# Eight unread matmuls after each post-norm sum, taken out of a one-core transformer kernel

## What is computed

```python
for l in range(DEPTH):    # DEPTH = 2
    h = h + 0.5 * rmsnorm(swiglu(rmsnorm(h, g_pre_ffn1[l]), w_ffn1_gu[l], w_ffn1_down[l]), g_post_ffn1[l])
    mix = token_mixer(rmsnorm(h, g_pre_mix[l]), ...)
    h = h + rmsnorm(mix, g_post_mix[l])
    h = h + 0.5 * rmsnorm(swiglu(rmsnorm(h, g_pre_ffn2[l]), w_ffn2_gu[l], w_ffn2_down[l]), g_post_ffn2[l])
```

## Time and profile before

| | us |
|---|---|
| median of three runs | 2387.8 |
| lowest, highest | 2387.32, 2390.79 |
| the profiled execution | 2391.2 |
| its span | 2389.7 |
| TensorE busy | 2335.6 (98%) |
| VectorE busy | 1629.8 (68%) |
| ScalarE busy | 1232.2 (52%) |
| mean granted clock of TensorE | 0.993 of full speed |
| HBM traffic | 159 GB/s over the span |

### The profile page before, as it was taken

How to read it: one execution, slowest core, us unless ns; L and a number is a source line. 1 busy time by engine, 2 the same in 40 slices (tenths; PEclk the granted TensorE clock), 3 DMA queues, 4 the chain that set the end, 5 groups by cost and what they waited for, 6 DMA issues and landing times.

```text
span 2389.7 us, 45375 instructions
## 1 busy us (share of the span) xinstructions
PE 2335.6 (98%) x18642; PEld 2283.4 (96%) x18642; DVE 1629.8 (68%) x2889; ACT 1232.2 (52%) x2050; POOL 61.8 (3%) x114
## 2 busy tenths in 40 slices
PE   8999999999999999999999999889999999989999
PEld 7999999999999999999999999889999999978999
DVE  6655987775486569788656875766765767574764
ACT  5444555554454445655445654555544645455542
POOL 2000200000000011000000000000000010000000
PEclk9999999999999999999999999899999999999999
DMA  7654634475556555447655655535755676533753
GB/s 200 186 177 127 169 98 124 131 194 177 169 159 177 177 148 131 106 142 189 186 188 160 185 187 155 141 89 142 201 187 171 181 200 191 158 93 89 203 187 132
DMA packets 583438, 382.77 MB, mean 160 GB/s; under 512 B 19977, under 2 KB 559091, under 8 KB 583232
## 3 DMA queue, kind: packets, MB, share of 16 engines
q1 hardware_dynamic: 580080, 376.78, 54.5%
q0 software_dynamic: 3152, 3.08, 0.5%
HBM read 378.67 MB, written 1.07 MB: 159 GB/s over the span
## 4 chain that ended last, share of the span: by engine, by line
PE 86%; DVE 8%; ACT 3%; issue 2%; DMA 1%; SPq 0%; DVEq 0%; ACTq 0%
PE bank L607 85%; DVE wlo L2040 1%; ACT whi L1347 1%; DVE ry L2059 1%; DVE ry L2057 1%; DVE a_qk L2602 0%; PE bank L938 0%; DVE ybuf L2090 0%; DVE smh L2476 0%; DMA wraw<-in_w_ffn_gu 0%; DVE hT L2094 0%; PE bank L706 0%; DMA wraw<-in_ffn_w_up 0%; DVE xlo L2073 0%; DVE ssum L2052 0%
## 5 line engine op out<-in xcount | busy, mean ns | idle before, releaser
L2040 DVE TENSOR_TENSOR wlo<-wraw,whi 128x1024 fp32r<-128x1024 f32 (+1 forms) x713 | 863.7, 1218 | 278.3 <-ACT whi L1347 274.3
L1347 ACT ACTIVATE whi<-wraw 128x1024 fp32r<-128x1024 f32 (+1 forms) x713 | 744.5, 1052 | 581.6 <-DMA wraw<-in_w_ffn_gu 168.5
L607 PE MATMUL bank<-xhi,whi 128*128 128x256 f32 (+2 forms) x3880 | 576.9, 288 | 7.3 <-ACT whi L1347 3.6
L607 PE MATMUL bank<-xhi,wlo 128*128 128x256 f32 (+2 forms) x3880 | 564.0, 285 | 6.1 <-DVE wlo L2040 6.1
L607 PE MATMUL bank<-xlo,whi 128*128 128x256 f32 (+2 forms) x3880 | 554.0, 284 | 0.0
L607 PEld LDWEIGHTS bank<-xhi,whi 128*128 128x128 f32 (+1 forms) x3880 | 511.1, 189 | 18.3 <-ACT xhi L1385 5.8
L607 PEld LDWEIGHTS bank<-xhi,wlo 128*128 128x128 f32 (+1 forms) x3880 | 509.6, 189 | 9.4 <-DVE wlo L2040 9.0
L607 PEld LDWEIGHTS bank<-xlo,whi 128*128 128x128 f32 (+1 forms) x3880 | 504.7, 188 | 0.2
L607 PE MATMUL bank<-act_hi,wlo 128*128 128x256 f32 (+1 forms) x1408 | 400.6, 284 | 0.0
L607 PE MATMUL bank<-act_lo,whi 128*128 128x256 f32 (+1 forms) x1408 | 400.5, 284 | 0.0
L607 PE MATMUL bank<-act_hi,whi 128*128 128x256 f32 (+1 forms) x1408 | 398.6, 283 | 0.0
(11 more groups left out here) (419 smaller groups left out, 1828.1 us busy)
## 6 DMA issues: line engine op xcount, KB each, us to landing
wraw<-in_w_ffn_gu SPq DMA_DIRECT2D x176, 512.0 KB, 3.9
wraw<-in_w_ffn_down SPq DMA_DIRECT2D x88, 512.0 KB, 3.2
wraw<-in_ffn_w_gate SPq DMA_DIRECT2D x88, 512.0 KB, 3.8
wraw<-in_ffn_w_up SPq DMA_DIRECT2D x88, 512.0 KB, 3.8
wraw<-in_ffn_w_down SPq DMA_DIRECT2D x88, 512.0 KB, 3.2
wraw<-in_w_in SPq DMA_DIRECT2D x80, 512.0 KB, 3.9
wraw<-in_a_w_in SPq DMA_DIRECT2D x26, 512.0 KB, 3.9
wraw<-in_w_out SPq DMA_DIRECT2D x16, 512.0 KB, 3.8
```

The source lines that it names most:

```text
L607: return E.matmul(out_, lhsT, rhs, start=first, stop=last, skip_group_check=True)
L1347: A.activation(flat(whi, u), flat(wraw, u), ACT.Copy).then_inc(S("hi"), 1)
L2040: V.tensor_tensor(flat(wlo, u), flat(wraw, u), flat(whi, u).bitcast(F32), ALU.subtract).then_inc(lo_ready[u % RING], 1)
```

## The change

The eight matmuls and the wait ahead of them are taken out of `stat`, with their constant. The sums themselves and all other instructions stay.

```diff
@@ -26,7 +26,6 @@
 RING = 7
 SLOT = 1024
 LEAD = 4
-AWAKE = 8
 HEAD = 4
 TAIL = 3
@@ -639,11 +638,6 @@
                 m = mm(bank[b][:, 0:n], C("mean1024"), sqb[:, 1, 0:n], False, True)
             m.then_inc(S("stat"), 1)
             c.norm += 1
-            if after is not None:
-
-                E.wait_ge(S("y"), KD * after + 2)
-                for _ in range(AWAKE):
-                    mm(bank[1][:, 0:n], C("mean1024"), C("ones")[:, 0:n], True, True)
 
         def head(slabs, x, fill, stat_at=None):
```

## The result

| | before | with the change |
|---|---|---|
| median, us | 2388.32 (4 runs, 2387.32 to 2390.79) | 2400.22 (4 runs, 2399.53 to 2402.09) |
| ratio, 95% interval | | 1.0044 [1.0033, 1.0056] |
| profiled execution, its span | 2391.2, 2389.7 | 2402.09, 2400.7 |
| mean granted clock | 0.993 | 0.986 |

The kernel is slower by 11.9 us (0.5%) in the medians and by 11.0 us in the span of the profiled execution. Forecast were 2399 us and +10.7. The change was run once more with the experiments, on another chip: 2402.08 against 2389.67 (21 runs), ratio 1.0050 [1.0038, 1.0063].

A forecast was written before the change was run, and what follows sets the result against it. TensorE was taken to bound the kernel, with 86% of the chain. Six low-clock stretches, 6 × 4.2 × 0.447 = 11.3, less 0.6, gave +10.7 us on the 2387.8 median: 2399 us, range 2394 to 2404.

The forecast's parts named there:

- The removed work is worth 0: At six post-norms, 48 unread matmuls, some 22.6 us of TensorE, lie hidden under the ScalarE and VectorE chain: 0 us.
- A fall at all six: At each of six post-norms, the new TensorE idle of 4.1 to 4.6 us drops the clock to 1.2 GHz.
- two waits that lost the clock: TensorE's waits for a_qm inside the mixers, 5.0 and 3.4 us, both followed by granted clock 0.5.
- 4.2 us of low work each: After each post-norm's idle, TensorE works 4.2 us at the low clock, the middle value taken.
- the long and the short kind: Low-clock stretches last about 6.8 or 3.4 us; expected work left after the idle: 5.0, or 3.4 or less.
- 0.447 a microsecond: Each microsecond of head work at the low clock loses 0.447 us, from eight matmuls taking 1.70 against 0.94 us.
- Heads are bound by TensorE, mixer heads give back 0.3: At low clock TensorE lags ScalarE's xhi supply, so heads lose time; two heads leading into mixers regain 0.3 us each.
- The clock didn't hold: Rival for the six post-norm idles: the clock stays at its upper level, price 0, 2388 us; chance 8%.
- The mixers absorbed next to nothing: Rival: two late heads leading into mixers cost nothing, so four post-norms pay 7.5 us, 2395.3 us; chance 12%.
- the third rival: Long low stretches at all post-norms, 5.0 to 6.8 us of low work: +12.8 to +17.6, 2400.6 to 2405.4 us; 15%.
- The signs: Expected in the profile after: long xhi waits, low clock reaching into the heads, wider matmul spacing, heads 1.5 to 2.5 us longer.

The follow-up runs named there:

- e5: Twelve unread matmuls instead of eight at each post-norm, against the kernel before the change; 2395.05 us, ratio 1.0027.
- e1: Four unread matmuls instead of eight at each post-norm, against the kernel before the change; 2390.78 us, ratio 1.0007.
- e8: Two unread matmuls instead of eight, waiting for ScalarE's Exp in mid-idle at each post-norm, against the kernel before the change; 2397.03 us, ratio 1.0036.
- e3: Eight unread matmuls kept behind the four FFNs, left out behind the two mixers, against the kernel before the change; 2391.91 us, ratio 1.0008.

## Why the prediction was right

- *The removed work is worth 0.* Right. All six heads start on the same wait for xhi, and the chain under it is as long as before. Its slack was larger than read, since the length of a merged row holds the last matmul's end (e5).
- *A fall at all six.* Right, in both profiles of the change. The reason behind it, that idles of 4.1 to 4.6 us lie between two waits that lost the clock, was good enough for this size. As a rule for shorter ones it fails: e1 with idles of 2.2 us or more and e8 with 1.1 and 1.75 us come out the other way round.
- *4.2 us of low work each*: the term that was undersized. It was 5.8, 4.7, 5.9, 5.8, 3.0 and 3.1 us, 4.75 in the mean. The choice between the long and the short kind in equal parts got four long ones to two. And the long ones lost less of themselves to the idle than said: the clock fell 2.3 to 3.1 us after the engine had stopped, not 2.5 at each, so they left 5.6 us of work in the mean instead of 5.0. In time: 12.7 instead of 11.3.
- *0.447 a microsecond.* Right. The heads are longer by 11.64 us, and 28.5 × 0.447 less 0.6 is 12.1. The factor of one half of the Trainium skill ("TensorE: Matmul & The Clock Gate", Terms), put on the same low work, would have given 13.7, further off.
- *Heads are bound by TensorE, mixer heads give back 0.3.* Right: 2.24 and 2.26 us of loss where the low work alone says 2.61.
- *Rivals.* The clock didn't hold. The mixers absorbed next to nothing: from the first mixer head's end to the next post-norm's head it took 222.28 us before (239.12 to 461.40) and 222.01 with the change (241.67 to 463.68), 0.3 us of a loss of 2.2; in the second mixer it was less than 0.1 us. Long stretches, said to be everywhere in the third rival, came at four of six.
- *What was luck.* The low work was sized too small by 1.4 us in sum, and the heads then lost 0.5 us less than it makes, and the rest of the kernel 0.6 less. So +10.7 stands closer to the +11.0 of the span than its terms do. The +12.4 of the second measurement, with more runs of the kernel before, is further off and still within the +9 to +13 that the forecast named.
- *The signs.* Six waits of about 4 us came with 24.6 us in sum (some 26 said), the mean clock at 0.986 (0.987 said), heads longer by 1.3 to 2.6 us (1.5 to 2.5 said), and 0.23 us between matmul starts with 272 columns (0.21 said).

## What to carry to other kernels

An engine that idles off the critical path can still cost, if its clock follows its work: before removing work that nobody reads, look at the granted clock behind waits of similar length in the same trace. Where TensorE bounds the stage after a dependency chain, a little filler under the chain pays. It needn't fill the wait: here four matmuls in the middle, 1.8 us from start to start, did as much as eight with 3.5 us; two were too few. And once such a price is known, look for other waits that pay it; here the fillings in the mixers won another 4 to 5 us.

## What the runs showed of the hardware

- The longest gap alone doesn't say whether the clock falls. In one profiled execution each, idles of 1.1 and 1.7 to 2.0 us around two matmuls lost it in five of six places, one idle of 2.2 to 2.6 us behind four matmuls in three of six (the slowest of eleven runs), and idles of 1.1 and 0.8 to 1.2 us around four matmuls in none (the third fastest of eleven). These runs don't give a rule for it.
- A low stretch is 3.4 or 6.8 us long in nearly every case of these profiles (once, in e1, 10.2). Which one it is can differ between kernels at the same place (3.4 and 6.8 us behind the second mixer in the change and in e3), while the two profiled executions of the change agree at all six post-norms. The runs of one kernel differ: before ranged over 7 us in 33 runs, with mean clocks of 0.992 to 0.996.
- Float32 transposes held a high clock as matmuls did (32 in a wait of 4.2 us, six of six places). Back to back one of 128 columns takes 0.11 us (16 more lengthen the row from 1.91 to 3.66), and each leaves one record, while a float32 matmul leaves two.
